# First layers of a model: squares summed where h is written, norms inside the products' blocks, and two latent products in one block

## The reference, cut to what matters

```python
def rmsnorm(x, g):
    y = x32 * lax.rsqrt(jnp.mean(x32 * x32, axis=-1, keepdims=True) + EPS)
    return (y * g.astype(jnp.float32)).astype(x.dtype)
...
nl = modulate(rmsnorm(hl, norm1_g[i]), mod_l[0], mod_l[1])     # n * (1 + scale) + shift
nc = modulate(rmsnorm(hc, norm1_g[i]), mod_c[0], mod_c[1])
# layer 0: pl = nl @ w_in; q = rmsnorm(pl[..:256]) @ w_uq; kv = rmsnorm(pl[256:384]) @ w_ukv
#          attention, short convolution, @ w_out
# layer 1: mLSTM mixer on nl @ w_in, nc @ w_in
hl = hl + mod_l[2] * yl
nl = modulate(rmsnorm(hl, norm2_g[i]), mod_l[3], mod_l[4])
hl = hl + mod_l[5] * peer(nl, ...)                             # experts by product keys
```

## Time and profile before

| | before |
|---|---|
| median of 3 runs | 4571.71 us |
| the profiled execution: its own time, its span | 4574.64 us, 4572.8 us |
| mean granted clock of TensorE | 0.944 |
| busy share PE, DVE, ACT, POOL | 89%, 72%, 44%, 25% |
| bytes moved, mean | 896 MB, 196 GB/s |

### The profile page before, as it was taken

The page is one execution under the profiler, slowest core; times in us unless marked ns, Lnnn a source line. Parts: engine busy times, 40 slices in busy tenths (PEclk is TensorE's granted clock), DMA queues, the critical chain, the costliest instruction groups (busy, mean ns, idle before and its releaser), DMA issues. The chain is left out here.

```text
span 4572.8 us, 74330 instructions
## 1 busy us (share of the span) xinstructions
PE 4079.0 (89%) x28272; PEld 3873.6 (85%) x28272; DVE 3281.0 (72%) x5802; ACT 2027.4 (44%) x3487; POOL 1155.1 (25%) x1007
## 2 busy tenths in 40 slices
PE   6777998999999997758999999799898999989898
PEld 4655998989999996638999999699788989978897
DVE  5866799778688886456987688666586676657666
ACT  5142333667433333324544454444464454446444
POOL 0000001667687882010039645200000000000000
PEclk8888998999999998878999999899899999989999
DMA  6403345898899994305776788654324545432453
GB/s 226 146 32 131 112 149 160 308 337 294 314 328 331 334 332 165 145 11 180 252 250 211 245 297 296 201 181 164 123 74 156 189 160 182 162 115 83 152 188 125
DMA packets 281607, 896.17 MB, mean 196 GB/s; under 512 B 29424, under 2 KB 73424, under 8 KB 278822
## 3 DMA queue, kind: packets, MB, share of 16 engines
q1 hardware_dynamic: 223286, 673.80, 43.5%
q0 software_dynamic: 55520, 201.60, 13.0%
q10 hardware_dynamic: 2448, 16.02, 0.9%
HBM read 834.92 MB, written 56.14 MB: 195 GB/s over the span
## 5 line engine op out<-in xcount | busy, mean ns | idle before, releaser
L153 DVE TENSOR_TENSOR weight_lo<-weight_ring,weight_hi 128x1024 fp32r<-128x1024 f32 x1084 | 1350.7, 1246 | 696.9 <-ACT weight_hi L148 679.0
L148 ACT ACTIVATE weight_hi<-weight_ring 128x1024 fp32r<-128x1024 f32 x1084 | 1143.1, 1055 | 1396.8 <-issue 727.1
L185 PE MATMUL pair0e_acc<-pair_xh,weight_hi 128*128 128x384 f32 (+1 forms) x1152 | 409.2, 355 | 10.4 <-ACT pair0e_gelu L2331 8.5
L185 PE MATMUL pair0e_acc<-pair_xl,weight_hi 128*128 128x384 f32 (+1 forms) x1152 | 398.5, 346 | 0.0
L185 PE MATMUL pair0e_acc<-pair_xh,weight_lo 128*128 128x384 f32 (+1 forms) x1152 | 398.2, 346 | 0.0
L185 PE MATMUL pair0e_acc<-pair0e_coef_hi,weight_hi 128*128 128x384 f32 x1024 | 343.5, 335 | 9.6 <-DVE pair0e_coef_lo L2056 9.5
L185 PE MATMUL pair0e_acc<-pair0e_coef_lo,weight_hi 128*128 128x384 f32 x1024 | 342.7, 335 | 0.0
L185 PE MATMUL pair0e_acc<-pair0e_coef_hi,weight_lo 128*128 128x384 f32 x1024 | 342.6, 335 | 0.0
L185 PE MATMUL peer10e_dot<-peer_xh,weight_hi 128*128 128x224 f32 (+1 forms) x1152 | 325.0, 282 | 8.7 <-DVE weight_lo L153 6.2
L185 PE MATMUL peer10e_dot<-peer_xl,weight_hi 128*128 128x224 f32 (+1 forms) x1152 | 318.2, 276 | 0.0
L185 PE MATMUL peer10e_dot<-peer_xh,weight_lo 128*128 128x224 f32 (+1 forms) x1152 | 318.1, 276 | 0.0
(11 more groups left out here) (618 smaller groups left out, 12382.0 us busy)
## 6 DMA issues: line engine op xcount, KB each, us to landing
weight_ring<-in_w_tiles SPq DMA_DIRECT2D x572, 512.0 KB
weight_ring<-in_peer_tiles SPq DMA_DIRECT2D x512, 512.0 KB
pair_acts<-pair0e_gelu SPq DMA_DIRECT2D x64, 384.0 KB
pair0e_act_in<-pair_acts SPq DMA_DIRECT2D x64, 384.0 KB
peer_acts<-peer10e_gelu SPq DMA_DIRECT2D x64, 224.0 KB
peer10e_act_in<-peer_acts SPq DMA_DIRECT2D x64, 224.0 KB
pair_coefs<-pair0e_G ACTq DMA_DIRECT2D x12, 1024.0 KB, 12.9
pair0e_kept_in<-pair_coefs SPq DMA_DIRECT2D x64, 192.0 KB
```

Of the source, the lines that this page charges most:

```text
L148: act.activation(self.tile_of(self.hi, g), self.ring[:, g % RING, :], ACT.Copy).then_inc(self.hi_done, 2)
L153: dve.tensor_tensor(self.tile_of(self.lo, g), self.ring[:, g % RING, :], self.tile_of(self.hi, g).bitcast(F32), ALU.subtract).then_inc(sel ...
L185: last = pe.matmul(out, lhsT, rhs, start=start and i == 0, stop=stop and i == len(passes) - 1, **more)
```

## The change

- `sums` [128, 512], the squares of `h` added over its 8 chunks, is kept in SBUF and made where `h` is written: in the modulation stage, in `even_out` and `odd_out` (`Squares`: ACT squares a chunk, DVE adds it), and at the end of the first experts.
- The norms before the experts take `sums`: one matmul instead of eight.
- `even_n` and `odd_n` are no stages any more: `Normed` computes the norm at the head of `even_in` and `odd_qk`, and PE waits for each k of job 0 (in `odd_qk` also of job 4, the first that needs the context columns) instead of for the whole norm.
- The norms of the latents run within `even_in` (`Latents`), on jobs 4 to 12.
- `even_uq` and `even_ukv` are one stage of 8 banks. ACT reads out partitions 0 to 63 (`beside`), DVE the rest; POOL copies the rotated keys into the 8 heads.
- The modulation rows of layer 0: before, 20 chunks in `even_in` and 12 in `even_out`; now 10, 12 in attention (24 dots) and 10.

```diff
         @block.tensor
         def _(pe):
             seen = None
+            if normed is not None:
+                normed.tensor(pe)
...
                 for i, ((lo, hi), part, passes, start, stop) in enumerate(j.mms):
+                    if normed is not None:
+                        normed.wait(pe, c, i)
...
+                    if beside is not None:
+                        act.wait_ge(*ready[c])
+                        beside(act, c, acc[:, c % banks, :]).then_inc(beside_done, 1)
...
+class Squares(Follow):
...
+    def scalar(self, act, c):
+        act.wait_ge(self.ready, c + 1)
+        if c >= 3:
+            act.wait_ge(self.added, c - 2)
+        out = self.sq[:, c % 2, :] if c else self.sums[:, 0:self.N]
+        act.activation(out, self.src(c), ACT.Square).then_inc(self.squared, 1)
+    def vector(self, dve, c):
+        dve.wait_ge(self.squared, c + 1)
+        if c:
+            if c >= 2:
+                dve.wait_ge(self.added, c - 1)
+            now = self.sums[:, 0:self.N]
+            dve.tensor_tensor(now, now, self.sq[:, c % 2, :], ALU.add).then_inc(self.added, 1)
...
+class Normed:
...
+        if by_stream:
+            self.pieces = [(c, i) for i in range(len(ranges)) for c in range(KD)]
+        else:
+            self.pieces = [(c, i) for c in range(KD) for i in range(len(ranges))]
...
+    def tensor(self, pe):
+        pe.matmul(self.total[:, :], self.ones, self.sums[:, :], start=True, stop=True).then_inc(self.summed, 1)
+    def wait(self, pe, job, k):
+        if (job, k) in self.needs:
+            pe.wait_ge(self.ready, self.needs[job, k])
...
+    def scalar(self, act):
+        act.wait_ge(self.meaned, 1)
+        act.activation(self.rstd[:, :], self.rstd[:, :], ACT.Sqrt).then_inc(self.rooted, 1)
+        for n, (c, i) in enumerate(self.pieces):
+            lo, hi, s = self.ranges[i]
+            act.wait_ge(self.scaled, n + 1)
+            act.activation(self.pair(c)[0][:, lo:hi], self.value[:, c, lo:hi], ACT.Identity,
+                           bias=self.shift(c, s)).then_inc(self.high, 1)
...
+    def vector(self, dve):
+        def low(n):
+            c, i = self.pieces[n]
+            lo, hi, s = self.ranges[i]
+            dve.wait_ge(self.high, n + 1)
+            dve.scalar_tensor_tensor(out=self.pair(c)[1][:, lo:hi], in0=self.value[:, c, lo:hi], scalar=self.shift(c, s),
+                                     in1=self.pair(c)[0][:, lo:hi].bitcast(F32), op0=ALU.add,
+                                     op1=ALU.subtract).then_inc(self.ready, 1)
...
+        dve.wait_ge(self.summed, 1)
+        dve.tensor_scalar(self.rstd[:, :], self.total[:, :], 1.0 / D, EPS, ALU.mult, ALU.add).then_inc(self.meaned, 1)
+        dve.wait_ge(self.rooted, 1)
+        seen = 0
+        for n, (c, i) in enumerate(self.pieces):
+            lo, hi, s = self.ranges[i]
+            if i >= seen:
+                seen += 1
+                dve.reciprocal(self.rstd[:, lo:hi], self.rstd[:, lo:hi]).then_inc(self.inverted, 1)
+                dve.wait_ge(self.inverted, seen)
+            dve.scalar_tensor_tensor(out=self.value[:, c, lo:hi], in0=self.h[:, c, lo:hi], scalar=self.scale(c, s),
+                                     in1=self.rstd[:, lo:hi], op0=ALU.mult, op1=ALU.mult).then_inc(self.scaled, 1)
+            if n >= 2:
+                low(n - 2)
+        low(len(self.pieces) - 2)
+        low(len(self.pieces) - 1)
...
+class Latents(Follow):
...
+    def scalar(self, act, c):
+        if c < 3:
+            act.wait_ge(self.ready, c + 1)
+            act.activation(self.sq[:, c, :], self.src[c], ACT.Square).then_inc(self.squared, 1)
+        if c == 6:
+            act.wait_ge(self.meaned, 2)
+            act.activation(self.rstd[:, :, :], self.rstd[:, :, :], ACT.Sqrt).then_inc(self.rooted, 1)
+        if c == 11:
+            for i in range(3):
+                act.wait_ge(self.scaled, i + 1)
...
+    def vector(self, dve, c):
+        if c == 5:
+            dve.wait_ge(self.summed, 1)
+            for i in range(2):
+                dve.tensor_scalar(self.rstd[:, i, :], self.total[:, i, :], 1.0 / ((2 - i) * P), EPS,
+                                  ALU.mult, ALU.add).then_inc(self.meaned, 1)
+        if c in (7, 8):
+            dve.wait_ge(self.rooted, 1)
+            dve.reciprocal(self.rstd[:, c - 7, :], self.rstd[:, c - 7, :]).then_inc(self.inverted, 1)
+        if c == 10:
+            dve.wait_ge(self.inverted, 2)
+            for i in range(3):
+                dve.scalar_tensor_tensor(out=self.sq[:, i, :], in0=self.src[i], scalar=self.gains[i],
+                                         in1=self.rstd[:, i // 2, :], op0=ALU.mult, op1=ALU.mult).then_inc(self.scaled, 1)
+        if c == 12:
+            for i in range(3):
+                dve.wait_ge(self.high, i + 1)
+                dve.tensor_tensor(self.pairs[i][1], self.sq[:, i, :], self.pairs[i][0].bitcast(F32), ALU.subtract)
...
-                pe.wait_ge(squared, c + 1)
-                last = pe.matmul(total[:, c // K, :], ones, sq[:, c, :], start=(c % K == 0), stop=(c % K == K - 1))
+            if sums is not None:
+                last = pe.matmul(total[:, 0, :], ones, sums, start=True, stop=True)
...
                         ins.then_inc(normed, 1)
+                if side is not None:
+                    side.dots(dve, s + 1, steps + 1)
+            if side is not None:
+                side.bias(dve)
...
                 for s in range(2):
...
+                    last = dve.scalar_tensor_tensor(out=h[:, n, s * T + SP:(s + 1) * T], in0=acc[:, n, s * OWN:(s + 1) * OWN],
+                                                    scalar=gate(n, s), in1=h_back[:, n, s * T + SP:(s + 1) * T],
+                                                    op0=ALU.mult, op1=ALU.add)
+                last.then_inc(written, 1)
+                if n >= 2:
+                    add(n - 1)
+            add(KD - 1)
...
+            for n in range(KD):
+                act.wait_ge(written, n + 1)
+                if n >= 3:
+                    act.wait_ge(added, n - 2)
+                out = sq[:, n % 2 * TT:(n % 2 + 1) * TT] if n else sums[:, :]
+                act.activation(out, h[:, n, :], ACT.Square).then_inc(squared, 1)
...
-                norm(nc, "even_n", lambda c: h[:, c, :], None, KD, TT, ones,
-                     lambda c, s: scales[:, 0, 0, s, c:c + 1], ranges=streams,
-                     shift=lambda c, s: modulation[:, 0, c, s:s + 1], pair=x)
+                normed = Normed(h, sums, ones, lambda c, s: scales[:, 0, 0, s, c:c + 1], lambda c, s: modulation[:, 0, c, s:s + 1],
+                                x, streams, False, {(0, k): 2 * k + 2 for k in range(KD)})
...
-                             side=ModulationRows(mod_rows, 0, range(EARLY, 36), c_rows, 2, modulation, cols))
+                             evacuated_out=done, normed=normed, follow=latents,
+                             side=ModulationRows(mod_rows, 0, range(EARLY, 26), c_rows, 2, modulation, cols))
...
+            assert last == first + 2
             with nc.sbuf_tensor("even_t2", [P, 2, TT], F32) as turn:
+                jobs = column_jobs(W, first, MLA_HEADS, 2, TT, split_pair(q_hi, q_lo))
+                jobs += [Job([((0, TT), 2 * last, W.stationary(2 * last, j * P, (kv_hi[:, :], kv_lo[:, :])), True, True)])
...
+                    c_kv = c - MLA_HEADS
+                    if c_kv >= MLA_HEADS // 2:
+                        return dve.tensor_copy(v[64:P, c_kv - MLA_HEADS // 2, :], ps[64:P, :])
+                    if c_kv >= 0:
+                        return dve.tensor_copy(k[0:64, 2 * c_kv + 1, :], ps[64:128, :])
                     chain(dve.tensor_tensor(turn[64:96, c % 2, :], ps[96:128, :], rope[96:128, :], ALU.mult))
                     chain(dve.tensor_tensor(q[64:96, c, :], ps[64:96, :], rope[64:96, :], ALU.mult))
-                    dve.tensor_copy(q[0:64, c, :], ps[0:64, :])
...
-            products(nc, W, "even_ukv", first, 1, jobs, keys_values, "vector")
+                def beside(act, c, ps):
+                    c_kv = c - MLA_HEADS
+                    if c_kv >= MLA_HEADS // 2:
+                        return act.activation(v[0:64, c_kv - MLA_HEADS // 2, :], ps[0:64, :], ACT.Copy)
+                    if c_kv >= 0:
+                        return act.activation(k[0:64, 2 * c_kv, :], ps[0:64, :], ACT.Copy)
+                    return act.activation(q[0:64, c, :], ps[0:64, :], ACT.Copy)
+                class Rotary(Follow):
+                    def gpsimd(self, pool):
+                        for head in range(MLA_HEADS):
+                            pool.tensor_copy(k[64:96, head, :], kr[64:96, :])
+                products(nc, W, "even_uqkv", first, 3, jobs, rotate, "vector", beside=beside, follow=Rotary(), banks=8)
...
-            attention(nc, "mla", units, ident)
+            attention(nc, "mla", units, ident, side=ModulationRows(mod_rows, 0, range(26, 38), c_rows, 2, modulation, cols))
...
```

(19 more changed lines are left out.)

156 lines of the change are left out of this document (102 added, 54 removed).

## The result

The changed kernel took **4503.5 us** (median of 4 runs, 4498.9 to 4515.7), the kernel before 4571.7: a ratio of **0.9855**, 95% interval 0.9841 to 0.9869. The forecast was 4510.4 with a range of 4500 to 4527, faster with 0.97. So the side and the range held; the gain is 68.2 us where 61.3 were summed. The profiled execution took 4504.8 us with a span of 4503.0, against 4572.8.

A forecast was written before the change was run, and what follows sets the result against it. Norms were taken as serial chains, latent products as bound by DVE's evacuations, attention by PE with DVE slack. Terms summed to -61.3 us from 4571.7, forecasting 4510.4 us, range 4500 to 4527.

The forecast's parts named there:

- Norms are chains, and their matmuls leave: At each norm, a serial chain holds up the next product; one matmul replaces eight, e.g. -7.7 before the first experts.
- The rival that pieces cost more: Both new norms: hand-overs of 0.15 us and job 1 entirely slow, +8, giving 4518 us; chance 0.14.
- The modulation stage, +0.4: Modulation stage: the added squares fall between weight tiles that DMA paces, +0.4 us (0 to 1.5).
- "In" product, -12.9, +2.6, -2.2: First norm and "in" product: earlier start -12.9, three full-precision matmuls for the latents' sums +2.6, shorter tail -2.2 us.
- Latents, block: Latents' norms leave as stages, -23.4 us; the two latent products become one block, -14.0 us.
- The block's four terms: Latent block: 2.9 us until the first job, 17.2 for query jobs, 5.4 for copies, 3.7 for weight tiles.
- the rival that POOL outlasts VectorE: Latent block: POOL blocks DVE (sum -55) or outlasts it at 5.6 us a copy (-45), 4517 to 4527; chance 0.14.
- The rule of the shared port: Latent block: two-SBUF-input DVE adds and POOL copies lock a shared port, each add waiting half a copy, 6 us.
- Attention, +10: Attention: 24 added dots exceed DVE's fillable idle time and wait for rows, +10 us (0 to 15).
- The rival by which slack suffices: Attention: DVE's idle time takes all the dots, sum -71, giving 4501 us; chance 0.10.
- Out products, +0.3 and +3.0: Even out product: 4 dots leave, 7 additions and a square come, +0.3; odd: 7 additions and a square, +3.0 us.
- The rival slower by the clock: "In" and odd products: thinly fed, PE stays at the low clock through dense jobs, +42, giving 4614 us; chance 0.02.

The follow-up runs named there:

- the run with the sums alone: Kernel before with only the running sums and one matmul per norm; norm stages, latents, blocks and modulation rows unchanged: ratio 0.9965.
- the whole norms: Changed kernel with the norms before the even in product and the odd product as stages of their own again, not fed by pieces: ratio 0.9887.
- the run with fewer dots: Changed kernel with even-layer rows spread anew; odd layer 12 dots in the v product, 4 instead of 10 in gate and out products: ratio 0.9854.
- a thinner feed: Changed kernel with an extra unused 0.40 us VectorE instruction behind 12 of 16 scalings of the first norm: ratio 0.9858.

## Why the prediction was right, and where it was off

The touched stages gave 70.0 us where 61.3 were summed, and the untouched ones took 0.2 back. The mechanism held in each stage. The sizes are mostly off in one direction, as prices were taken too high, and the time lies only 3.5 us above the range's lower end.

- *Norms are chains, and their matmuls leave.* Right, by each wait for a sum and by the run with the sums alone. The rival that pieces cost more falls with the whole norms, which cost 16.2 us more.
- *The modulation stage, +0.4.* Measured +1.0, and more in the other traces with the squares there.
- *"In" product, -12.9, +2.6, -2.2.* The sum's matmul came at 77.79 where 76.8 was forecast, and PE started 9.56 us behind it, where 9.5 were summed. Job 0 then took 11.1 us instead of 12.5 and made that up: the last k needs two low parts only and came 0.80 us behind the seventh, not 1.6, and the clock had risen. The charge of 1.0 for a slow job 1 was wrong, as the clock was up by then. What lies behind job 0 was forecast at +0.4 and measured +0.2.
- *Latents, block.* Both within 0.3 us. The block's four terms add up to 29.2, not to the 29.4 that the forecast went on with; from PE's first matmul at 189.03 to 218.02 it took 29.0. The copies' price on POOL was the mis-sized term, 0.56 us against 1.5 to 5.6: the rows that bounded it were another kind of instruction. Copies five times over, 28 us of them, still cost the block only 1.1 us, so the rival that POOL outlasts VectorE falls, and at 1.5 us a copy they would have been hidden too.
- *The rule of the shared port* was counted against the change at 6 us. It holds, but the copies are over when the additions begin.
- *Attention, +10.* Measured +8.2, and two terms were wrong. The dots were charged at their duration, 1.22 us, where the next instruction starts 1.14 behind (223.95 to 225.09): 1.8 too much for 22 dots. The waiting for rows, 2 to 3 us, did not come: the loads were issued at 219.16 and the first dot ran at 223.95 with no wait. Against that, the two last dots were not free but took 2.3 us, of which ACT's final copies hid 1.3. The 18 us of idle time were filled as forecast: 24 dots at 1.14 are 27.4, less 18.0 and 1.3. The rival by which slack suffices falls: DVE has no idle time left, and the stretch grew.
- *Out products, +0.3 and +3.0.* Measured -1.5 and +1.0. An addition cost 0.60 us in the even one and 0.34 in the odd one, not its duration, and the last square cost nothing, as dots stand in front of its addition. The changed kernel in the even one:

```profile
313.81 0.69 DVE L519 TENSOR_TENSOR sums<-sums,even_out_sq 128x512 f32<-128x512 f32 x1
314.41 1.22 DVE L856 CUSTOM_DVE_ANT_0 even_out_rows_junk<-even_out_rows,c_rows_sb 128x1024 f32<-128x1024 f32 x1
```

  The run with the sums alone, which keeps all 24 dots, agrees: its even out product, from the split on, takes 64.4 us instead of 60.2, seven additions of 0.60. The first row was waited for 0.3 us less (9.24 instead of 9.55; in the traces of the experiments that wait is 8.0 to 9.6). In the odd one a wait of 1.3 us for a row that stood before is gone; DVE paces it, but PE is close, as the run with fewer dots shows.
- *Clock.* The rival slower by the clock did not come about at this kernel's feed: at one k in 1.58 us the clock rose with the fifth k. Under a thinner feed it does stay down, but it was up with the third matmul of job 1, so even there it costs 1.5 us and not 100.
- *The untouched stages* differ by -2.6, +1.4 and +1.4, near nothing together.

## What to carry to other kernels

Where a norm feeds a product, add the squares up as the operand is written and hand the pieces over inside the product's block: both gains were there in full, and the pieces cost nothing here, with a k every 1.58 us where three matmuls take 1.28 at the low clock. Charge a VectorE instruction in a row of others with the distance to the next start (1.14 for a dot), not with its duration (1.22). When work is moved to fill an engine's idle time, compare the sum of its work with the stage's length, and expect only part of the idle time to be usable (9.4 of 15.9 us in one stage, but all 18 in attention). Where two engines are both busy nine tenths of a stage (attention: PE 58.2 and DVE 59.0 of 64.6 us), taking work off one gave back some six tenths of it.

## What was not expected of the hardware

- A GpSimd copy of 32x512 (fp32, SBUF to SBUF) takes 0.56 us, less than VectorE's 0.68 to 0.69 for an addition or a copy out of PSUM of that length, but more than the 0.41 that VectorE took for the very same copy before.
- In the lock between VectorE and GpSimd, GpSimd paid at every one of ten meetings (eight times about 0.5 us, twice 1.0), and at three of them VectorE's instruction was lengthened as well (by 0.52, 0.30 and 0.30 us).
- The clock rose while TensorE was still waiting for each k, at one k in 1.58 us, and did not at one in 2.38.
